# A hybrid layer kernel: the gate tiles of the GLA stage as pairs of seven products

## The chip, the cores and the metric

One core of a Trainium2 chip runs the whole program. The metric is the device time of one execution in microseconds (us); the median of three executions is taken.

## The reference, cut to what matters

One layer of a hybrid model for 320 tokens (256 of a prompt, 64 of a sample), all in float32. The input projection feeds three mixers (GLA, RWKV-7, Mamba-2) and three gates; the gated outputs are merged, projected, normalised and go through 64 experts.

```python
u = x @ w_in
u_gate, u_gla, u_rwkv, u_ssm = _split(u, (N_GATE, GLA_PROJ, RWKV_PROJ, SSM_PROJ))
o_gla, s_gla = _gla_mixer(u_gla, st_gla, gla_wa2, gla_ba, gla_norm_g)
...
g = jax.nn.sigmoid(u_gate.astype(jnp.float32)).reshape(b, l, 3, d)
merged = g[:, :, 0] * (o_gla @ gla_wo) + g[:, :, 1] * (o_rwkv @ rwkv_wo) + g[:, :, 2] * (o_ssm @ ssm_wo)
```

## The kernel before

The product `x @ w_in` is cut into NT = 115 tiles of 128 features by 320 tokens. The first 32 tiles are made ahead of the mixers, 28 of them as 14 pairs of seven products each (`project_pair`, L740): a 2 by 2 block scheme in which a pair of tiles takes seven block products of four 128x160 matmuls, not eight. GpSimd forms the sums of weight blocks for it (`weight_sums`), ScalarE copies four 160-column blocks out of the accumulators (`keep`), and VectorE adds the other blocks to them. The other tiles are made directly, as eight matmuls of 320 columns, between the steps of the mixers ("fill"), and ScalarE copies each whole tile out and stores it (`move`, L1463). The tile numbers run on: N_G0 = 96 to 98 are made between the Mamba-2 and the GLA stage, and the last 16 (99 to 114, all of them gate tiles) in the GLA stage.

The GLA stage (`gla(c)`, once in each of the engine programs) works through five chunks of 64 tokens, c = 0 to 4. Chunks 0 to 3 each carry four fill tiles; chunk 4 carries parts of the merge (`merge_part`, L1129). For one chunk:

- TensorE makes the pre-activation of the decays (L1065), turns the values (L1069), fills, makes and turns the scores' inputs (L1083, L1086), reads the state (L1093), applies the scores (L1101, signals `mixed`), makes the state's update (L1107), fills, and sums the squares for the norm (L1114).
- ScalarE copies the values (VT), moves a tile, then Exp and Ln of a softplus, three Exp for the decays (`decays`), moves a tile, Silu of the output gate, moves two tiles, and takes the square root of the norm (`root`, L1440).
- VectorE forms softplus's input, then its output (T4), a scan along the tokens (L2282), the difference EE (signals `gl_cs`), the scaled queries and keys (`gl_ops`), the masked scores (`gl_scm`), a copy and square of the output, the state (`gl_state`), the variance with a reciprocal (L2312), and five operations that normalise and gate the output (`gl_out`).
- SyncE loads the rows of the next chunk and the weights of a fill tile as soon as the slot's last tile is done.
- GpSimd forms six token sums for the merge at the start of the stage (`token_sums`, L2842 to L2846) and has nothing else there.

Each engine runs its own list in the written order and waits on semaphores. The order in which TensorE has its fill and the chunk's work is written out by hand:

```python
for f in range(3):
    fill(f)
...
pe.wait_ge(sem("gl_ops"), one)
...
last.then_inc(sem("state_sums"), 1)
fill(3)
```

## Time and profile before

| what | value |
|---|---|
| median of 3 executions | 1448.37 us (1446.8 to 1448.46) |
| the profiled execution's own time | 1444.06 us |
| its span | 1442.0 us |
| granted TensorE clock | 0.999 of full |
| busy: TensorE, VectorE, ScalarE, GpSimd | 98%, 50%, 29%, 16% |
| GLA stage, first TensorE work of chunk 0 | at 631.55 us |
| merge_part of chunk 4 begins | at 726.84 us |

The chain of work that ended last is followed back from the last instruction: each of its pieces released the next one. A piece on an engine other than TensorE is time in which TensorE had to wait. Busy shares are means over stages with different limits.

### The profile page before, as it was taken

What the parts mean: (1) busy time and instruction counts of PE and PEld (TensorE: products, weight loads), DVE (VectorE), ACT (ScalarE), POOL (GpSimd) and SP (SyncE); (2) the same over time, 40 slices, a digit from 0 to 9 for tenths busy, and PEclk for the clock granted to TensorE, in tenths of its full rate; (3) what the DMA queues carried; (4) which work ended last, traced back from release to release, by engine and by line L of the source; (5) the groups of instructions that cost most, each with busy time, mean ns of one, the idle gap of its engine ahead of it and who ended that gap; (6) DMA issues with size and microseconds to landing.
All of it is one profiled execution on the core that took longest, in us unless ns stands there. A gap on an engine that the chain in (4) does not pass through costs nothing.

```text
span 1442.0 us, 32350 instructions
## 1 busy us (share of the span) xinstructions
PE 1415.1 (98%) x13523; PEld 1024.3 (71%) x13523; DVE 724.3 (50%) x1360; ACT 411.3 (29%) x847; POOL 234.9 (16%) x193
## 2 busy tenths in 40 slices
PE   7999999999999999999999999999999999999997
PEld 6999777677777777667779985864476766757752
DVE  7443778887754677735458654623311112211217
ACT  2332543443432554434533211111111111111112
POOL 3784113230110111130013000011010000000000
PEclk9999999999999999999999999999999999999999
DMA  7796473744254444566568639699999999999996
GB/s 284 191 197 151 136 214 100 216 167 132 81 136 127 139 136 120 185 184 192 159 231 216 217 116 386 241 407 407 427 425 429 427 427 428 428 427 428 429 408 273
DMA packets 158017, 375.73 MB, mean 261 GB/s; under 512 B 102320, under 2 KB 110944, under 8 KB 139952
## 3 DMA queue, kind: packets, MB, share of 16 engines
q1 hardware_dynamic: 142048, 346.63, 67.2%
q0 software_dynamic: 7152, 16.85, 3.4%
q10 hardware_dynamic: 8672, 10.20, 2.0%
q8 instruction: 105, 1.72, 0.5%
q14 instruction: 40, 0.33, 0.1%
HBM read 329.22 MB, written 51.95 MB: 264 GB/s over the span
## 4 chain that ended last, share of the span: by engine, by line
PE 85%; DVE 6%; DMA 2%; ACT 2%; DVEq 2%; issue 1%; SPq 1%; ACTq 1%
PE PS L733 19%; PE PS L1303 15%; PE PS L1322 8%; PE PS L750 7%; PE PS L1149 6%; PE PS L1270 6%; PE PS L817 3%; PE PS L1129 2%; DVE region L1831 2%; PE PS L1191 2%; PE PS L1275 2%; DVE region L1838 2%; PE PS L1213 1%; DMA region<-projected 1%; PE PS L825 1%
## 5 line engine op out<-in xcount | busy, mean ns | idle before, releaser
L733 PE MATMUL PS<-h0T,region 128*128 128x320 f32 x1360 | 390.2, 439 | 2.0 <-issue 1.7
L1435 ACT ACTIVATE region<-PS 128x320 f32<-128x320 f32 (+5 forms) x351 | 145.7, 426 | 676.8 <-PE PS L733 237.6
L733 PEld LDWEIGHTS PS<-h0T,region 128*128 128x128 f32 x1360 | 251.2, 190 | 111.7 <-issue 15.0
L1303 PE MATMUL PS<-region 128*64 128x512 f32 x1024 | 228.1, 592 | 0.0
L1303 PEld LDWEIGHTS PS<-region 128*64 128x64 f32 x1024 | 117.6, 137 | 101.6 <-issue 49.8
L1831 DVE TENSOR_TENSOR region<-region 128x512 f32<-128x512 f32 (+10 forms) x237 | 165.3, 717 | 34.1 <-DMA region<-expert_rows 5.0
L1435 ACT ACTIVATE region<-region 128x256 f32<-128x256 f32 (+10 forms) x229 | 99.5, 465 | 83.0 <-DVEq L1854 13.7
L1322 PE MATMUL PS<-region,history 128*64 128x512 f32 x512 | 119.2, 597 | 1.1 <-ACTq L1771 0.5
L1831 DVE TENSOR_TENSOR history<-region,PS 128x256 f32<-128x256 f32 x32 | 13.5, 421 | 199.7 <-ACTq L1766 199.7
L1435 ACT ACT_TABLE_LOAD x77 | 98.8, 1283 | 25.3 <-ACTq L1482 9.8
L1838 DVE SCALAR_TENSOR_TENSOR region<-region,feature_vectors 128x320 f32<-128x320 f32 (+1 forms) x103 | 77.2, 750 | 53.2 <-ACTq L1511 41.0
L1270 PEld LDWEIGHTS PS<-region,h 128*128 128x128 f32 x736 | 85.8, 192 | 16.1 <-issue 15.9
L1270 PE MATMUL PS<-region,h 128*128 128x128 f32 x736 | 92.0, 278 | 0.0
L2565 DVE COPY region<-PS 128x512 f32<-128x512 f32 x32 | 22.1, 690 | 121.2 <-PE PS L1286 101.6
L1322 PEld LDWEIGHTS PS<-region,history 128*64 128x64 f32 x512 | 52.6, 137 | 42.5 <-issue 20.7
L1149 PE MATMUL PS<-region 128*128 128x160 f32 x528 | 73.8, 299 | 0.0
L1149 PEld LDWEIGHTS PS<-region 128*128 128x128 f32 x528 | 72.5, 190 | 0.2
L1435 ACT ACTIVATE region<-PS,region 128x512 f32<-128x512 f32 (+1 forms) x35 | 24.5, 699 | 146.7 <-PE PS L1322 146.4
L750 PE MATMUL PS<-region 128*128 128x160 f32 x448 | 65.4, 299 | 0.0
L750 PEld LDWEIGHTS PS<-region 128*128 128x128 f32 x448 | 62.4, 190 | 0.0
L1831 DVE TENSOR_TENSOR region<-region,PS 128x160 f32<-128x160 f32 (+3 forms) x95 | 43.3, 488 | 34.4 <-PE PS L750 14.7
L817 PEld LDWEIGHTS PS<-region 64*64 64x64 f32 x2720 | 49.8, 134 | 14.9 <-issue 12.7
(250 smaller groups left out, 1576.2 us busy)
## 6 DMA issues: line engine op xcount, KB each, us to landing
region<-moe_w SPq DMA_DIRECT2D x65, 2048.0 KB, 30.3
region<-moe_w SPq DMA_DIRECT2D x65, 1024.0 KB, 29.3
region<-w_in SPq DMA_DIRECT2D x115, 512.0 KB, 5.7
region<-wo SPq DMA_DIRECT2D x32, 512.0 KB, 4.3
expert_rows<-region SPq DMA_DIRECT2D x20, 512.0 KB, 7.2
region<-expert_rows SPq DMA_DIRECT2D x5, 2048.0 KB, 17.3
projected<-region ACTq DMA_DIRECT2D x59, 167.5 KB, 4.0
region<-projected SPq DMA_DIRECT2D x10, 768.0 KB, 6.8
```

The lines of the kernel that those rows point to most:

```text
L733: last = mm(PS[:, 6 + i % 2, 0:NTOK], WR[:, i, k, :], H0T[:, k, :], start=(k == 0), stop=(k == KT - 1))
L750: last = mm(out, lhs(k), rhs(k), start=start and k == 0, stop=k == KH - 1, skip_group_check=True)
L817: last = mm(head(out(j), 1 - x if across and j > 3 else x), head(lhs(j), x), head(rhs(j), x), **kw)
L1129: last = mm(PS[:, b, 0:NTOK], WR[:, i, k, :], OT[:, 8 * q + k, :], start=(k == 0 and q < 3), stop=(k == KT - 1 and q != 2))
L1149: last = mm(out, lhs(k), rhs(k), start=start and k == 0, stop=k == KH - 1, skip_group_check=True)
L1191: last = mm(PS[:, 2 * t + h, :], MG[:, k, t * 128:t * 128 + 128], WOUT[:, k, h * 512:h * 512 + 512], start=(k == 0), stop=(k == KT - 1))
L1270: last = mm(bank(h, 4, 128)[:, k], H0[:, t, (4 * h + k) * 128:(4 * h + k) * 128 + 128], OH[:, p, t, :], start=(h == 0 and k == 0 and t == ...
L1303: last = mm(PS[tiles(i), 2, :], XE[:, k, tiles(i)], W13[r][i][:, k * 512:k * 512 + 512], start=(k == 0), stop=(k == KT - 1))
L1322: last = mm(PS[tiles(i), 5 + h, :], HIDT[:, f, tiles(i)], W2[r][i][:, f * D + h * 512:f * D + h * 512 + 512], start=(f == 0), stop=(f == 1))
L1435: return nc.scalar.activation(out, in_, f, **kw)
L1831: return dve.tensor_tensor(out, a, b, op)
L1838: return dve.scalar_tensor_tensor(out=out, in0=a, scalar=s, in1=b, op0=op0, op1=op1)
```

## The change

The 16 gate tiles of the GLA stage become GATE_PAIRS = 8 pairs of seven products, two pairs in each of the chunks 0 to 3.

- TensorE: `gate_pair(g, first, end)` issues products first to end of pair g. Products 1, 3 and 6 go to block X (bank 6), 2 and 4 to Z (first half of bank 7), 5 and 7 to W (its second half); there is one set of blocks, so each pair waits for VectorE to have read the last one's. In a chunk, products 1 to 6 of the even pair stand behind L1065, product 7 and products 1 to 5 of the odd pair behind L1069, and products 6 and 7 of the odd pair behind L1107. Products 1 and 2 of pair 0 stand ahead of the chunk's first step.
- ScalarE: each `move` of a tile is replaced by copies of 160 columns (`keep_gate`), four to a pair. Two stand ahead of the root, which is moved from the end of its chunk into the next one, two behind softplus's Exp, two behind the decays, two ahead of Silu. The copy of VT moves behind the decays.
- VectorE: three adds to a pair (`gate_first`, `gate_rest`, `gate_last`). The last block of the even pair is added between T4 and the scan. Softplus's input of the next chunk (`gate_decays(c + 1)`) is formed ahead of the wait for the root.
- GpSimd: sums of weight blocks for each pair (`gate_sums`, four operations of 512 columns), with the token sums of the merge behind those of pair 1 and pair 3. A copy of the token sums TSUM into GTOK (2560 columns) is added in the first chunk of the Mamba-2 stage.
- SyncE: loads two tiles at a time, one pair's tiles once the slots are free, and issues the stores too, which ScalarE issued before. Tiles 99 and 100 are loaded ahead of the stage.

```diff
+        GTOK = take(4, KT // 2, NTOK // 2)
+        GSUM = [take(4, KT // 2, 128) for _ in range(2)]
...
-            weights((N_GLA - 1) // RING, (N_GLA - 1) % RING)
+            for n in range(N_GLA - 1, N_GLA + 2):
+                weights(n // RING, n % RING)
...
+            def gate_weights(g):
+                n = gate_tiles(g)[0]
+                for m in (n, n + 1):
+                    weights(m // RING, m % RING)
+            def gate_stores(g):
+                n, a, b = gate_tiles(g)
+                sp.wait_ge(sem("added_out"), 3 * g + 3)
+                for m, i in ((n, a), (n + 1, b)):
+                    sp.dma_start(ut[TILE[m], :, :, :], STG[:, i, :, :]).then_inc(sem(f"store_done{i}"), 16)
...
             gla_rows(0)
-            gla_weights(0)
+            gate_weights(1)
             gla_rows(1)
-            for c in range(1, NPC):
-                gla_rows(c + 1)
-                gla_weights(c)
+            for c in range(NPC - 1):
+                gate_weights(2 * c + 2)
+                gate_stores(2 * c)
+                gate_weights(2 * c + 3)
+                gla_rows(c + 2)
+                gate_stores(2 * c + 1)
...
+            def gate_pair(g, first, end):
+                p = PAIRS + g
+                n, a, b = gate_tiles(g)
+                X, Z, W = gate_blocks()
+                def product(k, out, lhs, rhs, start):
+                    for j in range(KH):
+                        last = mm(out, lhs(j), rhs(j), start=start and j == 0, stop=j == KH - 1, skip_group_check=True)
+                        if k == 5 and j < 2:
+                            last.then_inc(sem("tile_done"), 1)
+                    last.then_inc(sem("quad"), 1)
+                for k in range(first, end + 1):
+                    if k == 1:
+                        for m, i in ((n, a), (n + 1, b)):
+                            pe.wait_ge(sem(f"weights_in{i}"), (m // RING + 1) * 16)
+                        if g > 0:
+                            pe.wait_ge(sem("added_out"), 3 * g - 1)
+                        else:
+                            pe.wait_ge(sem("tile_moved"), N_GLA + 2)
+                        product(k, X, lambda j: WR[:, a, j, :], lambda j: H0H[:, j, 0], True)
+                    if k == 2:
+                        if g > 0:
+                            pe.wait_ge(sem("added_out"), 3 * g)
+                        product(k, Z, lambda j: WR[:, b, KH + j, :], lambda j: GTOK[:, 3, j], True)
+                    if k == 3:
+                        pe.wait_ge(sem("weights_summed"), p + 1)
+                        pe.wait_ge(sem("quad_kept"), 4 * p + 1)
+                        product(k, X, lambda j: GSUM[g % 2][:, 1, j], lambda j: GTOK[:, 1, j], False)
+                    if k == 4:
+                        pe.wait_ge(sem("quad_kept"), 4 * p + 2)
+                        product(k, Z, lambda j: WR[:, a, KH + j, :], lambda j: H0H[:, KH + j, 0], True)
+                    if k == 5:
+                        product(k, W, lambda j: GSUM[g % 2][:, 0, j], lambda j: GTOK[:, 0, j], True)
+                    if k == 6:
+                        pe.wait_ge(sem("quad_kept"), 4 * p + 3)
+                        product(k, X, lambda j: GSUM[g % 2][:, 2, j], lambda j: GTOK[:, 2, j], False)
+                    if k == 7:
+                        pe.wait_ge(sem("quad_kept"), 4 * p + 4)
+                        pe.wait_ge(sem("added_out"), 3 * g + 1)
+                        product(k, W, lambda j: GSUM[g % 2][:, 3, j], lambda j: H0H[:, KH + j, 1], False)
...
+                if c is not NPC:
+                    gate_pair(2 * c, 1 if c > 0 else 3, 6)
...
+                if c is not NPC:
+                    gate_pair(2 * c, 7, 7)
+                    gate_pair(2 * c + 1, 1, 5)
...
-                fill(3)
+                if c is not NPC:
+                    gate_pair(2 * c + 1, 6, 7)
...
+            def keep_gate(g, made, x):
+                act.wait_ge(sem("quad"), 7 * (PAIRS + g) + made)
+                a_(GKEPT[:, x].rearrange("p (c w) -> p c w", c=NCH), tuple(gate_blocks())[(0, 0, 1, 2)[x]], ACT.Copy)
+                act.drain().then_inc(sem("quad_kept"), 1)
             def gla(c):
-                def fill(f):
-                    if c is not NPC:
-                        move(c * (FILL_G // RING) + (N_GLA + f) // RING, (N_GLA + f) % RING)
-
-                one = c + 1
+                one, pairs = c + 1, c is not NPC
...
-                act.wait_ge(sem("gl_out"), one)
-                act.wait_ge(sem("gl_v"), 2 * NCH + one)
-                a_(VT, bank(1, 4, 128), ACT.Copy)
-                act.drain().then_inc(sem("gl_vt"), 1)
-                fill(0)
+                if pairs:
+                    keep_gate(2 * c, 1, 0)
+                    keep_gate(2 * c, 2, 2)
+                if c > 0:
+                    root(RG4, "variance", NCH + c, "rstd")
                 act.wait_ge(sem("softplus_in"), NCH + one)
                 a_(LB4, AB4, ACT.Exp, scale=-1.0)
-                act.drain()
+                if pairs:
+                    keep_gate(2 * c, 3, 1)
+                    keep_gate(2 * c, 5, 3)
+                else:
+                    act.drain()
                 a_(LB4, LB4, ACT.Ln, bias=1.0)
                 act.drain().then_inc(sem("softplus_out"), 1)
                 act.wait_ge(sem("gl_cs"), one)
...
                 a_(EE, EE, ACT.Exp, scale=1.0 / 16)
                 act.drain().then_inc(sem("decays"), 1)
-                fill(1)
+                if pairs:
+                    keep_gate(2 * c + 1, 1, 0)
+                    keep_gate(2 * c + 1, 2, 2)
+                act.wait_ge(sem("gl_out"), one)
+                act.wait_ge(sem("gl_v"), 2 * NCH + one)
+                a_(VT, bank(1, 4, 128), ACT.Copy)
+                act.drain().then_inc(sem("gl_vt"), 1)
+                if pairs:
+                    keep_gate(2 * c + 1, 3, 1)
+                    keep_gate(2 * c + 1, 5, 3)
                 a_(RR, UG[:, 16:24, :], ACT.Silu)
                 act.drain().then_inc(sem("gate_silu"), 1)
-                fill(2)
-                fill(3)
-                root(RG4, "variance", NCH + one, "rstd")
+                if c is NPC:
+                    root(RG4, "variance", NCH + one, "rstd")
...
-            def gla(c):
-                one = c + 1
+            def gate_decays(c):
                 dve.wait_ge(sem("gl_pre"), c * 2 + 1)
                 tt(T4, bank(0, 4, L, n=256), vec(V_BA, 4, L), add)
                 dve.drain()
                 stt(AB4, T4, -1.0, T4, mul, mx)
                 dve.drain().then_inc(sem("softplus_in"), 1)
+            def gate_first(g):
+                p, (n, a, b), (X, Z, W) = PAIRS + g, gate_tiles(g), gate_blocks()
+                dve.wait_ge(sem("quad_kept"), 4 * p + 4)
+                dve.wait_ge(sem(f"store_done{a}"), (n // RING + 1) * 16)
+                tt(quad_out(a, 0), GKEPT[:, 0].rearrange("p (c w) -> p c w", c=NCH), Z, add)
+                dve.drain().then_inc(sem("added_out"), 1)
+            def gate_rest(g):
+                p, (n, a, b), (X, Z, W) = PAIRS + g, gate_tiles(g), gate_blocks()
+                dve.wait_ge(sem("quad"), 7 * p + 6)
+                dve.wait_ge(sem("quad_kept"), 4 * p + 4)
+                dve.wait_ge(sem(f"store_done{b}"), ((n + 1) // RING + 1) * 16)
+                tt(STG[:, b, :, HIST:CW].rearrange("p c (j w) -> p j c w", j=2), GKEPT[:, 2:4].rearrange("p x (c w) -> p x c w", c=NCH),
+                   X.unsqueeze(1).to_broadcast([128, 2, NCH, L // 2]), add)
+                dve.drain().then_inc(sem("added_out"), 1)
+            def gate_last(g):
+                p, (n, a, b), (X, Z, W) = PAIRS + g, gate_tiles(g), gate_blocks()
+                dve.wait_ge(sem("quad"), 7 * p + 7)
+                tt(quad_out(a, 1), GKEPT[:, 1].rearrange("p (c w) -> p c w", c=NCH), W, add)
+                dve.drain().then_inc(sem("added_out"), 1)
+            def gla(c):
+                one, pairs = c + 1, c is not NPC
+                if pairs:
+                    gate_first(2 * c)
+                    gate_rest(2 * c)
                 dve.wait_ge(sem("softplus_out"), NCH + one)
 
...
+                if pairs:
+                    gate_last(2 * c)
                 flat = lambda x: x.rearrange("p a b -> p (a b)")
                 dve.tensor_tensor_scan(flat(CS4), CON[:, C_RST:C_RST + 4 * L], flat(T4), 0.0, mul, add)
                 dve.drain()
...
                 dve.drain().then_inc(sem("gl_ops"), 1)
+                if pairs:
+                    gate_first(2 * c + 1)
                 dve.wait_ge(sem("gl_pre"), c * 2 + 2)
...
                 dve.wait_ge(sem("state_sums"), NCH + one)
                 tt(SG, SG, banks(1, 2, 4, 256), add)
                 dve.drain().then_inc(sem("gl_state"), 1)
+                if pairs:
+                    gate_rest(2 * c + 1)
+                    gate_last(2 * c + 1)
                 dve.wait_ge(sem("square_sums"), NCH + one)
...
                 dve.reciprocal(RG4, RG4)
                 dve.drain().then_inc(sem("variance"), 1)
+                if pairs:
+                    gate_decays(c + 1)
...
+            gate_decays(0)
...
+                if c == 0:
+                    pool.tensor_copy(GTOK, TSUM)
+                    pool.drain()
...
-            for q in (0, 2):
-                token_sums(q)
+            def gate_sums(g):
+                n, a, b = gate_tiles(g)
+                S1, S2, S3, S4 = (halves(GSUM[g % 2][:, x]) for x in range(4))
+                A11, A12, A21, A22 = (halves(WR[:, i, k * KH:k * KH + KH, :]) for i in (a, b) for k in range(2))
+                for m, i in ((n, a), (n + 1, b)):
+                    pool.wait_ge(sem(f"weights_in{i}"), (m // RING + 1) * 16)
+                if g > 1:
+                    pool.wait_ge(sem("quad"), 7 * (PAIRS + g - 1))
+                ptt(S1, A21, A22, add)
+                ptt(S3, A11, A21, sub)
+                pool.drain()
+                ptt(S2, S1, A11, sub)
+                pool.drain()
+                ptt(S4, A12, S2, sub)
+                pool.drain().then_inc(sem("weights_summed"), 1)
+            for g in range(GATE_PAIRS):
+                gate_sums(g)
+                if g in (1, 3):
+                    token_sums(g - 1 if g == 3 else 0)
```

## Rows read from the trace of the kernel before

**Rows 1.** page, part 1: busy us of each engine (share of the span) and instructions.

```profile
PE 1415.1 (98%) x13523; PEld 1024.3 (71%) x13523; DVE 724.3 (50%) x1360; ACT 411.3 (29%) x847; POOL 234.9 (16%) x193
```

**Rows 2.** chain that ended last, GLA stage: start us, us, engine, what it made, line.

```profile
624.47 6.84 DMA region<-projected
...
631.55 0.69 PE PS L1065 x16
...
656.53 13.12 PE PS L733 x48
...
672.02 1.06 PE PS L1107 x8
673.09 4.50 PE PS L733 x16
677.59 0.86 PE PS L1114 x4
...
679.07 0.88 PE PS L1069 x16
679.94 13.12 PE PS L733 x48
...
726.84 13.12 PE PS L1129 x48
```

**Rows 3.** timeline of chunk 1: start us, us, engine, line, operation [idle before, releaser].

```profile
661.96 1.28 ACT L1435 ACT_TABLE_LOAD   x1 [0.45 <-ACTq L1482]
...
663.73 1.28 ACT L1435 ACT_TABLE_LOAD   x1
...
665.99 0.69 DVE L2282 TENSOR_TENSOR_SCAN region<-constants,region 128x256 f32<-128x256 f32 x1
...
667.24 1.03 ACT L1435 ACTIVATE region<-region 128x256 f32<-128x256 f32 x3 [0.43 <-DVEq L2285]
...
668.66 0.75 DVE L1831 TENSOR_TENSOR region<-region 128x256 f32<-128x256 f32 x2
...
669.57 0.31 PEld L1083 LDWEIGHTS PS<-region 128*64 128x64 f32 x8 [0.44 <-DVEq L2291]
...
672.86 2.04 DVE L1831 TENSOR_TENSOR region<-region 128x512 f32<-128x512 f32 x2
...
674.98 1.22 DVE L1831 TENSOR_TENSOR region<-region,PS 128x1024 f32<-128x1024 f32 x1
...
678.99 1.75 DVE L2312 RECIPROCAL region<-region 128x256 f32<-128x256 f32 x1
```

**Rows 4.** the same chain where pairs of seven products run, 14 and 12 pairs.

```profile
34.71 106.49 PE PS L750 x784
...
766.37 91.28 PE PS L1149 x672
```

**Rows 5.** timeline where pairs run: matmuls, a copy, an add.

```profile
96.48 2.34 PE L750 MATMUL PS<-region 128*128 128x160 f32 x16
96.69 0.30 ACT L1435 ACTIVATE region<-PS 128x160 f32<-128x160 f32 x1 [2.96 <-PE PS L750]
...
103.21 0.32 DVE L1831 TENSOR_TENSOR region<-region,PS 128x160 f32<-128x160 f32 x1 [0.16 <-PE PS L750]
```

**Rows 6.** issues of the fill tiles' weights, 606 to 704 us.

```profile
DMA to landing us min/median/max: 5.0/6.5/7.8
```

**Rows 7.** timeline, end of the Mamba-2 stage: the last three direct tiles and a token sum.

```profile
617.25 13.16 PE L733 MATMUL PS<-h0T,region 128*128 128x320 f32 x48 [0.26 <-ACTq L1482]
...
622.72 1.54 POOL L2842 TENSOR_TENSOR region<-region 128x640 f32<-128x640 f32 x1 [7.93 <-DVEq L376]
```

**Rows 8.** timeline, VectorE with and without GpSimd beside it.

```profile
178.49 2.01 DVE L1831 TENSOR_TENSOR region<-region,constants 128x512 f32<-128x512 f32 x1
178.72 1.23 POOL L2771 TENSOR_TENSOR region<-region,feature_vectors 128x512 f32<-128x512 f32 x1
...
202.56 0.69 DVE L1831 TENSOR_TENSOR region<-region,constants 128x512 f32<-128x512 f32 x1
```

More of the change, by code:

```diff
@@ L39 @@
 UNITS = 12
+GATE_PAIRS = 8
 UNIT_ORDER = (0, 2, 3, 1)
@@ L209, in quad_sum, with gate_tiles, gate_blocks @@
             return shaped(PS[:, b, 0:NTOK // 2], NCH, L // 2)
+        def gate_tiles(g):
+            n = N_GLA + 2 * g
+            return n, n % RING, (n + 1) % RING
+        def gate_blocks():
+            return (shaped(PS[:, b, o:o + NTOK // 2], NCH, L // 2) for b, o in ((6, 0), (7, 0), (7, NTOK // 2)))
         def kept(u, x):
@@ L232, in hybrid_layer @@
         RG = take(4, L)
+        ssm_end = at[0]
         assert at[0] <= REGION.shape[1], at[0]
@@ L245, in hybrid_layer @@
         UAS = (UA, UA2)
+        at[0] = mixer_end + 24 * L
+        GKEPT = take(4, NTOK // 2)
+        gates_at = 31872
+        assert at[0] <= 27776 and ssm_end <= gates_at
+        at[0] = gates_at
+        GTOK = take(4, KT // 2, NTOK // 2)
+        GSUM = [take(4, KT // 2, 128) for _ in range(2)]
+        assert at[0] <= 36864 + 768 + KT * 128
         at[0] = mixer_base
@@ L567, in gla_rows @@
                 sp.dma_start(UGS[c % 2], ut[T_GLA:T_GLA + 24, :, c, HIST:CW].rearrange("t p w -> p t w")).then_inc(sem(landed), 16)
-            def gla_weights(c):
-                for f in range(FILL_G):
-                    weights(c * (FILL_G // RING) + (N_GLA + f) // RING, (N_GLA + f) % RING)
+            def gate_weights(g):
[7 more added lines that the diff above has]
+                    sp.dma_start(ut[TILE[m], :, :, :], STG[:, i, :, :]).then_inc(sem(f"store_done{i}"), 16)
             def gla_out(s):
@@ L600, in _ @@
                 mixer_weights(0, n % RING, n + 1)
+                if n == NT - RING + 1:
+                    gate_stores(GATE_PAIRS - 2)
+            gate_stores(GATE_PAIRS - 1)
             gla_out(0)
@@ L1070, in gla @@
                 last.then_inc(sem("gl_v"), 1)
-                for f in range(3):
-                    fill(f)
+                if c is not NPC:
+                    gate_pair(2 * c, 7, 7)
+                    gate_pair(2 * c + 1, 1, 5)
                 if c is NPC:
-                    pe.wait_ge(sem("tile_moved"), NT + 1)
+                    pe.wait_ge(sem("added_out"), 3 * GATE_PAIRS)
                     merge_part(0, 0, 7)
-                    pe.wait_ge(sem("tile_moved"), NT + 2)
                     merge_part(0, 2, 6)
@@ L1660, in _ @@
                 move(n // RING, n % RING)
+            def keep_gate(g, made, x):
+                act.wait_ge(sem("quad"), 7 * (PAIRS + g) + made)
+                a_(GKEPT[:, x].rearrange("p (c w) -> p c w", c=NCH), tuple(gate_blocks())[(0, 0, 1, 2)[x]], ACT.Copy)
+                act.drain().then_inc(sem("quad_kept"), 1)
             def gla(c):
-                def fill(f):
-                    if c is not NPC:
-                        move(c * (FILL_G // RING) + (N_GLA + f) // RING, (N_GLA + f) % RING)
-                one = c + 1
+                one, pairs = c + 1, c is not NPC
                 act.wait_ge(sem(gla_in(c)[0]), gla_in(c)[1])
                 UG = UGS[c % 2]
-                act.wait_ge(sem("gl_out"), one)
-                act.wait_ge(sem("gl_v"), 2 * NCH + one)
-                a_(VT, bank(1, 4, 128), ACT.Copy)
-                act.drain().then_inc(sem("gl_vt"), 1)
-                fill(0)
+                if pairs:
[3 more added lines that the diff above has]
+                    root(RG4, "variance", NCH + c, "rstd")
                 act.wait_ge(sem("softplus_in"), NCH + one)
                 a_(LB4, AB4, ACT.Exp, scale=-1.0)
-                act.drain()
+                if pairs:
[3 more added lines that the diff above has]
+                    act.drain()
                 a_(LB4, LB4, ACT.Ln, bias=1.0)
@@ L1705, in keep_unit @@
             def keep_unit(u, made, x, region):
-                act.wait_ge(sem("quad"), 7 * (PAIRS + u) + made)
+                act.wait_ge(sem("quad"), 7 * (PAIRS + GATE_PAIRS + u) + made)
                 a_(UKEPT[u % 2][:, 160 * x:160 * x + 160], region, ACT.Copy)
@@ L2348, in unit_sums @@
             def unit_sums(u):
-                p = PAIRS + u
+                p = PAIRS + GATE_PAIRS + u
                 ring, (a, b), _ = unit_weights(u)
@@ L2834, in _ @@
                 pool.drain().then_inc(sem("squares_summed"), 1)
+                if c == 0:
+                    pool.tensor_copy(GTOK, TSUM)
+                    pool.drain()
             meet(pool, 3)
```

8 lines of the change are left out of this document (4 added, 4 removed).

## The prediction, made before the change was run

> **What bounds the kernel now.** I read the page first, then the chain of waits, then the timeline of one GLA chunk. The page shows TensorE busy for 98% of the span [rows 1], so a saving on it counts wherever nothing else takes its place. The chain through the GLA stage is almost all TensorE [rows 2]: one chunk's three fill tiles begin at 656.53, the next chunk's at 679.94, a period of 23.41 us. Of it 13.12 + 4.50 = 17.6 us are the four tiles and 5.8 us the chunk's own steps. But the timeline shows a second chain right behind: VectorE ends the operations before `gl_ops` at 668.66 + 0.75 = 669.41, and TensorE's first weight load after its three tiles starts at 669.57, put down to them [rows 3]. ScalarE and VectorE have almost no slack against 13.12 us of fill. The question is therefore not only what the products save, but which hand-overs the shorter fill still hides.
>
> **What the products save.** A direct tile takes 13.12 / 3 = 4.37 us [rows 2], a pair of tiles 8.75. Seven products take 106.49 / 14 = 7.61 us and 91.28 / 12 = 7.61 us where pairs run elsewhere, 1.09 a product [rows 4]. That is 1.14 us a pair, 2.3 a chunk, 9.1 us over eight pairs if TensorE never waits. Nothing else moves off TensorE.
>
> **A steady chunk, step by step.** Zero is the start of L1107 (672.02 in chunk 1 [rows 2]). A hand-over from TensorE to a copy takes 0.21, the copy 0.30, its signal 0.05 [rows 5], and TensorE starts 0.16 after a signal [rows 3].
>
> 1. L1107 (1.06), products 6 and 7 of the odd pair (2.17) and L1114 (0.86) end at 4.1. The next L1065 waits for the state. Square and decayed state end at 674.90, the state's add runs 674.98 to 676.20 [rows 3], that is 4.18, plus 0.16: 4.34. Loss 0.2. Before, the 4.50 us tile hid this.
> 2. L1065 ends at 4.96, product 1 at 6.05, product 2 at 7.13. ScalarE's second copy is out at 7.7.
> 3. Now ScalarE has the root and softplus's Exp ahead of the third copy. Both need a table load, and loads follow the last operation directly, then the operation: one load to the next is 1.77 us [rows 3]. Two of them end at 11.24; the third copy's signal is at 11.6, TensorE can start product 6 at 11.75. It ended product 5 at 4.96 + 5 x 1.09 = 10.4. Loss 1.35. VectorE's variance is no cause: its adds and the 1.75 us reciprocal [rows 3] end near 7.6, ahead of the root.
> 4. Products 6, L1069 (0.88), 7: to 14.8. The add of the last block waits for product 7 (0.2) and takes 0.32 [rows 5]; the scan starts at 15.4. From the scan's start to the end of the three Exp was 665.99 to 668.27, 2.28 us [rows 3]: 17.7. Only then does ScalarE copy the odd pair's first block: signal at 18.05, product 3 at 18.2. Products 1 and 2 had ended at 17.0. Loss 1.2.
> 5. Products 3 to 5 (3.26) and L1083 to L1101 (2.38 before, from the end of the 13.12 us to 672.02 [rows 2]) end at 23.85. VectorE's `gl_ops` come near 18.9, hidden; `gate_first` ahead of the masked scores ends before L1086 does.
>
> So the period is 23.85 where it was 23.41: 2.3 us saved, 2.75 lost to the three waits. ScalarE's copies by themselves are cheap (8 x 0.30 against four copies and stores) and its issue of stores goes to SyncE; it is their place in its list that costs. SyncE's stores wait for `added_out`, with the loads of the next odd pair and of rows behind them. These weights land 5.0 to 7.8 us after issue [rows 6] and are wanted some 15 us after, so I price SyncE's new order at nothing; without that cover each late load would be TensorE's wait one to one.
>
> **Entry and exit.** Tile 98 ends at 630.4 and L1065 started at 631.55, after the rows had landed at 631.3 [rows 2, 7]. Now tile 98 is copied out (631.1) and products 1 and 2 run ahead, to 633.3. Up to L1107 there are then L1065, ten more products (10.9), L1069, the loss at product 3 (1.25) and the 2.38: 649.3, where chunk 0 had 648.6. That is +0.7. Three steady periods (chunk 0 to 3) give 3 x 0.44 = +1.3. Out of chunk 3 the merge began 7.92 after L1107 (679.94 less 672.02, the same in each chunk [rows 2]); now it is 4.34 + 0.62 + 0.88 = 5.84: -2.1. Chunk 4's own chain is hidden by 13.12 us of merge [rows 2], since its root no longer follows any copy. Sum so far: -0.1 us.
>
> **GpSimd beside VectorE.** Before, GpSimd had only the token sums, at the start of the stage. Now it has 32 operations of 512 columns in it. A VectorE operation with both inputs in SBUF took 2.01 us where a GpSimd one ran 178.72 to 179.95 beside it, and 0.69 alone [rows 8]: it ended 0.55 after GpSimd's, +1.3 us. Adds that read PSUM kept their 0.32 [rows 5]. The Trainium skill ("GPSIMD Engine Reference", Specifications) says the same and more: VectorE's two-port modes, which have one SBUF input, contend too. By that rule the two scaling operations of the normalisation would be hit as well, and the sum below would be some 0.6 higher.
>
> Where do the hits lie on the path? Weights of the next even pair are issued at product 5 (9.6 after zero) and land 6.5 later [rows 6], at 16.1, against scan and difference at 15.4 to 16.7; a pair's sums last about 5.3 us. I take half a hit, 0.6, in chunk 1 and in chunk 2; chunk 3 has none. In chunk 0 the sums of pair 1 (weights from 637, until 642.5) lie on scan and difference (from 640.9): 1.3. Then come three token sums of 1.54 [rows 7] and pair 2's sums, until about 652.5, on the square and the decayed state of chunk 0, which now set the next L1065: 1.3. The token sums behind pair 3 lie on the normalisation of chunk 0's output, ahead of `gate_first` of chunk 1: 0.7. Sum 4.5. Bounds: 0, if every hit falls into slack, and 9, if a hit goes through two GpSimd operations in a row (S1 and S3 have no gap between them). I take 4.5, since the row shows the hit plainly and its places are on the path, and the two bounds lie equally far.
>
> The copy into GTOK (2560 columns on GpSimd in the Mamba-2 stage) has no row of its length. Five times the 512-column rows is 6 us [rows 8]; it stands where GpSimd is idle until its next turn. Between 0 and one hit (1.3) is its cost; I take 0, the operations on the path there read PSUM.
>
> **Sum.** -0.1 + 4.5 = +4.4 us. The profiled execution took 1444.06 for a span of 1442.0, 4.3 below the median of 1448.37. Against its own time the sum is 1448.5, against the median 1452.8. I give the latter. About 0.2% (2.9 us) is what a measurement of this kernel can tell from no change.
>
> **Rivals.**
>
> - *The waits, without the hits* (0.27). GpSimd's sums fall into slack, up to a microsecond of them counts: 1448.3 to 1449.3. For it: 2.4 us of slack on `gl_ops`, and the second batch of sums in a steady chunk meets operations that read PSUM. Against it: chunk 0, where sums and token sums queue up for 15 us.
> - *Longer hits* (0.10). Each goes through two GpSimd operations: +9, 1457.
> - *Faster: ScalarE is in time for product 6* (0.14). If the root's table load ran ahead of the first two copies, in the time in which ScalarE waits for them, the third copy would come at 10.3, and the loss of 1.35 would go in three chunks: -4.1, so 1444.2 without hits. For it: ScalarE is idle then. Against it: in the trace loads stand right ahead of their operation, behind the copies [rows 3]. It decides the sign from 0.9 us less loss a chunk on, if the hits are absent too. All losses gone would be -9.1, 1439.3, which no row supports.
> - *The forecast* (0.45), with its own range of 1450.5 to 1455.5.
>
> The rest (0.04) I leave to places that I have not seen, on the slow side.
>
> Faster by over 0.2%: 0.14. Within 0.2%: the second case less a part that it gives to the slow side, plus a little of the forecast's lower end: 0.28. Slower: 0.58. The range goes from 1446.5, which leaves out the faster case, to 1457.5, which takes in the longer hits' estimate.
>
> **What would show each step.** In the changed profile the products' line should be about 1.09 us a product; TensorE's idle time should stand ahead of the product's matmuls with ScalarE as its releaser, some 1.2 us four times and 1.35 three times, and 0.2 ahead of L1065 with VectorE. The period of chunk 3 should be near 23.9 and those of chunks 1 and 2 longer. The merge should begin near 731 against 726.84. Scan, difference or the decayed state should show over 1 us where they had 0.42 to 0.69 or 1.22. The prediction is wrong if the idle time at product 6 is missing (table loads placed elsewhere), if VectorE's operations keep their lengths (no hits), or if TensorE waits for weights.

## The result, and the profile after

The changed kernel took **1460.07 us** (median of 4 runs, 1458.64 to 1460.9) against 1447.59 before (4 runs, 1444.44 to 1448.46): ratio **1.0089, 95% interval 1.0071 to 1.0108**. It is slower by 12.5 us, where +4.4 was forecast; 1460 lies above the forecast's range. The profiled execution took 1460.9 for a span of 1459.1.

Part 1 of the page, which answers to [rows 1]:

```profile
PE 1414.4 (97%) x13715; PEld 1041.1 (71%) x13715; DVE 746.8 (51%) x1384; ACT 413.6 (28%) x863; POOL 278.8 (19%) x226
```

TensorE's busy time is where it was (1415.1 before), in a span 17 us longer. Of these 17 us 2.4 stand ahead of the GLA stage, in this pair of profiles: 0.7 of them before any changed work (the row of 64 matmuls at 448.82 before starts at 449.48 here), and in the second profiles of both kernels (experiments 11 and 12) the stage starts only 0.4 us apart. I don't count them to the change. To place the loss I measure the *stage*: from the end of tile 98 to the start of chunk 4's merge. It was 96.4 us before (630.41 to 726.8); now it is 109.1 (632.80 to 741.9), +12.7. The period from one state update to the next (L1107 before, L1183 now) was 23.4 three times and is 28.07, 27.87 and 24.66.

The chain of waits of the changed kernel, chunks 1 and 2 (L1094 the products, L1183 the state update, L1139 the old L1065, L1512 ScalarE, L1922, L1926 and L2405 VectorE's adds, scalings and scan):

```profile
665.10 1.27 DVE region L1922
...
668.13 1.47 DVE region L1926
...
671.32 1.34 PE PS L1094 x8
...
673.13 1.51 DVE region L2405
...
674.72 1.25 DVE region L1922
...
677.63 3.50 PE PS L1094 x24
...
683.51 1.07 PE PS L1183 x8
684.58 2.37 PE PS L1094 x16
686.95 0.86 PE PS L1191 x4
...
687.87 0.69 PE PS L1139 x16
...
688.57 2.43 PE PS L1094 x16
...
691.41 1.28 ACT L1512
...
693.21 1.28 ACT L1512
...
695.18 1.35 PE PS L1094 x8
...
699.32 1.51 DVE region L2405
...
700.92 1.26 DVE region L1922
...
703.83 5.17 PE PS L1094 x24
```

Before, this chain was TensorE's almost alone [rows 2]. Now it leaves TensorE at two of the places that the prediction named: two table loads ahead of product 6 (it starts at 695.18, 11.67 after the zero of 683.51; 11.75 was forecast), and scan, difference and Exp ahead of product 3 of the odd pair. Three things differ from the forecast. Scan and difference take 1.51 and 1.26 in *both* chunks, against 0.69 [rows 3] and 0.42; half of one such hit was forecast for a chunk. The normalisation ahead of `gate_first` is stretched by more than the 0.7 forecast (1.27 and 1.47 at 665 to 669.6), and holds TensorE to 671.32. And the three products at 703.83 take 5.17 us, those at 677.63 3.50; nothing of that was forecast.

Here are chunk 3's rows of the same chain, where no sums of GpSimd are left:

```profile
727.19 0.69 DVE region L2405
...
727.96 0.42 DVE region L1922
...
730.17 3.50 PE PS L1094 x24
```

The granted clock (the first column after the engines' busy times), in stretches around three products each:

```profile
647.90:653.10 5.20, 5.20 (x26) 5.03 (x28) 2.03 (x3) 1.13 (x3) 4.83 (x4) 0.67 0.05 9
677.60:681.10 3.50, 3.46 (x26) 3.33 (x26) 1.69 (x2) 1.17 (x3) 1.07 (x1) 1.00 0.01 2
703.80:709.00 5.20, 5.17 (x26) 5.03 (x28) 1.68 (x2) 1.17 (x3) 1.07 (x1) 0.67 0.00 0
```

Twice TensorE ran part of the three products at its lower level (a mean of 0.67 between 1.2 and 2.4 GHz), behind 2.40 and 2.81 us without work; once, behind 2.81 too, it didn't. Each fall cost 1.67 us.

Behind the stage there is one more difference, at the first unit of the mixer (L1226):

```profile
785.41 3.53 PE L1226 MATMUL PS<-region 128*128 128x160 f32 x24 [1.76 <-DVEq L2495]
```

### The profile page after: what moved, and what is told of

Its sections match the earlier page's. It is cut to its first block, busy times and chain, and to the rows that moved or that the text cites. A ratio compares the mean times of both kernels' runs of the same rounds, so it can differ in the third digit from the quotient of the medians.

```text
span 1459.1 us, 32888 instructions
## 1 busy us (share of the span) xinstructions
PE 1414.4 (97%) x13715; PEld 1041.1 (71%) x13715; DVE 746.8 (51%) x1384; ACT 413.6 (28%) x863; POOL 278.8 (19%) x226
## 3 DMA queue, kind: packets, MB, share of 16 engines
q8 instruction: 107, 1.75, 0.5%
## 4 chain that ended last, share of the span: by engine, by line
PE 82%; DVE 8%; ACT 3%; DMA 2%; DVEq 2%; issue 1%; SPq 1%; ACTq 1%
PE PS L766 15%; PE PS L1380 15%; PE PS L1399 8%; PE PS L783 7%; PE PS L1226 6%; PE PS L1347 6%; PE PS L1094 3%; DVE region L1922 3%; PE PS L850 3%; PE PS L1268 2%; PE PS L1352 2%; DVE region L1929 2%; PE PS L1290 1%; ACT region L1512 1%; ACT L1512 1%
## 5 line engine op out<-in xcount | busy, mean ns | idle before, releaser
L1512 ACT ACTIVATE region<-PS 128x160 f32<-128x160 f32 (+6 forms) x367 | 148.3, 415 | 673.9 <-PE PS L766 207.6
L766 PE MATMUL PS<-h0T,region 128*128 128x320 f32 x1104 | 319.3, 439 | 2.4 <-issue 2.1
L766 PEld LDWEIGHTS PS<-h0T,region 128*128 128x128 f32 x1104 | 203.1, 190 | 91.2 <-issue 14.0
L1922 DVE TENSOR_TENSOR region<-region 128x512 f32<-128x512 f32 (+10 forms) x237 | 173.8, 752 | 35.7 <-DMA region<-wo 5.9
L1512 ACT ACTIVATE region<-region 128x256 f32<-128x256 f32 (+10 forms) x229 | 99.5, 465 | 93.7 <-DVEq L2408 14.3
L1922 DVE TENSOR_TENSOR history<-region,PS 128x256 f32<-128x256 f32 x32 | 13.5, 421 | 199.0 <-ACTq L1857 199.0
L1347 PEld LDWEIGHTS PS<-region,h 128*128 128x128 f32 x736 | 85.8, 192 | 16.1 <-issue 15.9
L1922 DVE TENSOR_TENSOR region<-region,PS 128x160 f32<-128x160 f32 (+4 forms) x119 | 52.3, 466 | 58.5 <-ACTq L1743 16.4
L1226 PE MATMUL PS<-region 128*128 128x160 f32 x528 | 74.1, 299 | 1.8 <-DVEq L2495 1.8
L1226 PEld LDWEIGHTS PS<-region 128*128 128x128 f32 x528 | 72.5, 190 | 2.2 <-DVEq L2495 2.0
L1512 ACT ACTIVATE region<-PS,region 128x512 f32<-128x512 f32 (+1 forms) x35 | 24.5, 699 | 146.7 <-PE PS L1399 146.4
L3032 POOL DMA_INDIRECT expert_rows<-region,row_index x21 | 20.6, 983 | 233.1 <-DVEq L2728 233.1
```

The source lines that it names most:

```text
L766: last = mm(PS[:, 6 + i % 2, 0:NTOK], WR[:, i, k, :], H0T[:, k, :], start=(k == 0), stop=(k == KT - 1))
L1226: last = mm(out, lhs(k), rhs(k), start=start and k == 0, stop=k == KH - 1, skip_group_check=True)
L1347: last = mm(bank(h, 4, 128)[:, k], H0[:, t, (4 * h + k) * 128:(4 * h + k) * 128 + 128], OH[:, p, t, :], start=(h == 0 and k == 0 and t == ...
L1512: return nc.scalar.activation(out, in_, f, **kw)
L1922: return dve.tensor_tensor(out, a, b, op)
```

## The experiments

My theory after the result: of the 12.7 us of the stage, most is GpSimd's sums beside VectorE's short chain, with the lower clock behind the longer waits, and the rest the order of ScalarE's copies. The rival: the order of the work alone (copies behind table loads, the chunk's first products behind L1139), with GpSimd beside the point. Line numbers of the variants lie a few above those of the changed kernel.

**1. No sums by GpSimd from pair 2 on** (the sums of pairs 0 and 1 are used for all, so the gates are not the reference's), and **2. no sums at all** (nor are the ones of pairs 0 and 1 made; the token sums stand at the stage's start).

```diff
+                if g > 1:
+                    nc.gpsimd.sem_inc(sem("weights_summed"), 1)
+                    return
```

> This kernel leaves out GpSimd's sums of weight blocks for the pairs 2 to 7 (it waits for the weights and signals at once; TensorE multiplies by the sums of pairs 0 and 1), so the gates are not the reference's; everything else keeps its place. Read the GLA stage alone, from the end of the last direct tile to the start of chunk 4's merge: 96.4 us before, 109.1 in the changed kernel. Theory (GpSimd's sums stretch VectorE's two-input operations, and these lie on the path): in chunks 1 and 2 the scan and the difference go from 1.51 and 1.26 us back to 0.69 and 0.42, the stage falls by 1.65 twice, and the clock's dip in chunk 2 goes as well (1.7): 104.1. Rival (the stretching has another cause, the order on ScalarE say): both operations stay at 1.5 and 1.26 and the stage at 109.

> This kernel leaves out all of GpSimd's sums of weight blocks (the places hold other numbers, copied there in the Mamba-2 stage) and has the token sums at the stage's start as the kernel before, so that GpSimd does nothing beside VectorE from chunk 0's middle on. Theory (ScalarE's order costs about 1.3 us a period, the rest is GpSimd): all periods fall to that of chunk 3 of the changed kernel, 24.7 us, the first part to 19.5 (22.6 less 1.2 for the stretched operations and 1.9 for the clock): stage 99.4 against 109.1, so 9.7 of the 12.7 us are GpSimd's and 3.0 ScalarE's order. Rival (the hits fall into slack and the order on ScalarE costs it all): stage 107 or more.

Measured: 1451.21 and 1450.50 us; the kernel before took 1446.7 beside them. The stages are 100.4 and 99.3 us, all periods 24.54 to 24.67, and no clock below 1.00 around the products. Each of the runs up to the sixth is one execution; I read them by the stage in its profile. In the second run other numbers stand in the places of the sums, so its gates aren't the reference's either. The rival falls. All but 3 us of the 12.7 go with the sums, the clock's part among them. The first came out better than expected (100.4, not 104) for two reasons: TensorE was idle for 2.27 us in chunk 0, behind the one stretched difference that was left, and its clock held (1.7); and with no sums of pairs 2 and 3 ahead of them the token sums were over at 661.4, before the normalisation, which was no longer stretched (1.9).

**3. Third copy ahead of softplus's Exp, 4. the odd pair's first copy ahead of the decays, 5. both.**

```diff
+                if pairs:
+                    keep_gate(2 * c, 3, 1)
                 act.wait_ge(sem("softplus_in"), NCH + one)
...
+                if pairs:
+                    keep_gate(2 * c + 1, 1, 0)
                 act.wait_ge(sem("gl_cs"), one)
```

> One thing is moved: ScalarE's third copy of the even pair stands between the root and softplus's Exp, not behind the Exp. Theory (product 6 waits only because one more table load stands ahead of that copy; but what ends the chunk is the scan, behind T4): TensorE's wait ahead of product 6 falls from about 1.3 us to nothing in chunks 2 and 3, product 7 comes 1.2 earlier, yet T4 comes 0.35 later, so the scan gains only some 0.5: the wait ahead of product 3 of the odd pair grows by 0.7, and a period falls by 0.5. Stage 107.5. Rival (a wait taken away is worth its length): a period falls by 1.3, stage 105.

> One thing is moved: ScalarE's first copy of the odd pair stands ahead of its wait for the scan (gl_cs), not behind the three Exp of the decays. Theory (product 3 of the odd pair waits for that copy alone): the wait ahead of product 3 goes, product 4 waits for the second copy, 1.1 us of the wait are won in each of four chunks, and TensorE's longest idle stretch falls from 2.6 to 1.5 us, so that the two dips of the clock go (1.7 and 1.9): stage 109.1 - 4.4 - 3.6 = 101.1. Rival (the dips do not come from the idle time): they stay, stage 104.7. Second rival (the chain of VectorE ends the chunk anyway): the wait moves to L1159 and the stage stays at 109.

> Both moves of ScalarE's copies together: the third copy of the even pair ahead of softplus's Exp, the first copy of the odd pair ahead of the wait for the scan. Alone they gave a stage of 106.1 and 103.9 us against 109.1. Theory (each removes another wait of TensorE, and what is left are VectorE's stretched operations): the gains add, stage 101. Rival (one chain through scan and decays holds both, so the second move finds the same wait): 103 or more.

Measured: 1457.71, 1455.56 and 1451.79 us; stages of 106.1, 103.9 and 101.8. The waits that the prediction ascribed to ScalarE's list are ScalarE's: without sums beside it (chunk 3) the period is 23.64 with the one copy moved, 24.46 with the other, and 23.25 with both, 1.4 less than in the changed kernel. While the sums lie on VectorE's chain the gain is less regular (28.73 in chunk 1 of the first, where the clock fell behind a wait of 3.05), since the waits go to the next hand-over. None of the three came out as forecast. The first took 1.0 off the clean period, between my 0.5 and the rival's 1.3. The second was worse than I expected (101, measured 103.9): the falls of the clock went, but the copy gave 0.2 in the clean chunk and not 1.1, because product 4 of the odd pair then waited for the second copy (1.05 us, and 1.6 beside the sums). The third was expected at 101.

**6. Only GpSimd's work moved**: the even pairs' sums wait for `gl_ops`, the odd pairs' for `gl_state`, the token sums for the state of chunk 3.

```diff
+                    if g % 2 == 0:
+                        pool.wait_ge(sem("gl_ops"), g // 2)
+                    else:
+                        pool.wait_ge(sem("gl_state"), (g + 1) // 2)
...
-                if g in (1, 3):
-                    token_sums(g - 1 if g == 3 else 0)
+            pool.wait_ge(sem("gl_state"), NPC + 1)
+            for q in (0, 2):
+                token_sums(q)
```

> The changed kernel with GpSimd's work moved in time alone: the sums of an even pair wait for gl_ops (scan and decays are over), those of an odd pair for gl_state, the token sums for the state of chunk 3. Theory (what costs is where the sums meet VectorE, not that they are there): scan and difference keep 0.69 and 0.42 us in chunks 1 and 2, the square and decayed state grow by about 1 us in chunks 0 to 2; of the 9.8 us that went with all sums left out, some 6 come back: stage 103.5. Rival (two engines at work cost the same wherever the sums are put): stage 108 or more.

Measured: 1451.21 us, stage 99.5, periods 24.55, 24.54 and 24.67. I had expected 103.5, with square and decayed state stretched; they kept 2.04, since the even pair's sums were over (676.84) before the square began (677.45). The same work of GpSimd, done elsewhere in the chunk, costs 0.2 us against no sums at all (99.3, run 2). Its chain in chunk 2 reads as chunk 3 of the changed kernel did:

```profile
692.42 0.69 DVE region L2405
...
693.19 0.42 DVE region L1922
...
695.28 3.50 PE PS L1094 x24
```

**7. Both copies, the odd pair's second copy too, and the sums moved. 8. As 7, with VectorE making S1 and S3 of the even pairs**, GpSimd S2 and S4, and VT's transposes right behind L1139.

> Third copy of the even pair ahead of Exp, first and second copy of the odd pair ahead of the scan's wait, and GpSimd's sums placed as in the run before. Theory: TensorE waits only for the state at a chunk's start (by 1.0 us, since the even pair's sums lie on the square and the decayed state) and in chunk 0, a period is 21.4 + 0.8 for the starts of groups + 0.8 = 23.0, stage 17.9 + 3 x 23.0 + 5.9 = 93, that is 3 us less than before the change, and the time 1446 to 1447 against some 1447.5. Rival (gl_ops come late, hit by the same sums): the wait moves to L1159, a period is 24 and the time is 1450.

> As the run before, with two more steps: VectorE makes two of the four sums of an even pair between gl_ops and its masked scores (GpSimd the other two), and TensorE turns the values right behind L1139, so that products 6 and 7 stand together. Theory: GpSimd's part no longer lies on the decayed state (0.8 us a period less) and one start of a group less (0.2): period 22.0, stage 90 to 91, time 1444. Rival (VectorE's two sums delay the masked scores by more than they save): period 23 or more, a wait ahead of L1177.

Measured: 1449.25 us (10 runs; ratio to before 1.0007, interval 0.9995 to 1.0019) and 1452.59 (6 runs; 1.0033, 1.0018 to 1.0047). I had expected periods near 23 and 22; they are 24.19 three times, and 24.71, 25.05, 23.74. VectorE and TensorE in the timeline of run 7:

```profile
698.29 0.45 PE L1159 MATMUL PS<-region 128*64 128x64 f32 x8 [0.72 <-DVEq L2415]
...
706.56 0.69 PE L1139 MATMUL PS<-region 128*64 128x64 f32 x16 [1.52 <-DVEq L2434]
```

```profile
701.58 3.51 DVE L1923 TENSOR_TENSOR region<-region 128x512 f32<-128x512 f32 x2
```

Square and decayed state took 3.51 us together where they had 2.04 [rows 3], with the even pair's sums beside them, and L1139 waits for the state behind them. The earlier copies had shortened the chunk so far that this became the path. The wait at L1159 has another cause: the second copy now stands ahead of the decays' table load. In run 8 VectorE's own two sums (1.29 us for both) are put into the chain directly: TensorE waits 0.90 us at L1177, ahead of which they stand, as that run's rival had it. Both are misses.

**9. Run 5 with the sums moved as in run 6. 10. The same, with the last four stores issued by ScalarE.**

```diff
-                if n == NT - RING + 1:
-                    gate_stores(GATE_PAIRS - 2)
-            gate_stores(GATE_PAIRS - 1)
...
+            act.wait_ge(sem("added_out"), 3 * GATE_PAIRS)
+            for g in (GATE_PAIRS - 2, GATE_PAIRS - 1):
+                n, a, b = gate_tiles(g)
+                for m, i in ((n, a), (n + 1, b)):
+                    act.dma_start(ut[TILE[m], :, :, :], STG[:, i, :, :]).then_inc(sem(f"store_done{i}"), 16)
```

> Third copy ahead of the softplus Exp and the odd pair's first copy ahead of the decays (as in the run with both copies moved), the odd pair's second copy behind the decays as in the changed kernel, and GpSimd's sums in the slack (even pairs' once KET's operands are made, odd pairs' once the state is updated). Theory: without hits of GpSimd every period is what the last one of the run with both copies was, 23.25 us, so the stage is 95.5 us (99.5 less three times 1.3) and the time about 1448.3: within 0.2% of the kernel before. Rival: the even pair's sums, which stretched the square and the decayed state in the run with three copies moved, come onto the path here too: periods of 24.2 and more, stage 98, time 1450 or more.

> The run above with one thing more: the four stores of the last two pairs are issued by ScalarE at the start of chunk 4 instead of by SyncE among the loads of wo. Theory: the wait of 1.6 to 1.8 us at the first unit's third product comes from gate rows that land 1.0 us later because they share SyncE's queue with the stores; with the stores on ScalarE's queue the first gate rows land within 4.0 to 4.3 us of issue again and the time is 1.0 to 1.7 us below the run above, about 1447. Rival: the wait stays within 0.3 us, since it comes of GpSimd's token sums beside VectorE's unit sums and of where the loads meet other transfers; the time is the same as above within 0.3.

Measured: run 9 took **1447.93 us** (12 runs, 1446.43 to 1449.71) against 1449.6 before beside it (23 runs): ratio 0.9986, interval 0.9974 to 0.9998. Its median is the lowest of the variants (run 10 is as good within the noise), 12 us below the changed kernel and level with the one before (the gain of 0.14% is less than the 0.2% that I count). Its stage is 96.5 us (95.5 expected), its periods 23.66 (23.25 expected; square and decayed state take 2.44 there for 2.04, beside the end of the even pair's sums). The timeline of TensorE in one period of it:

```profile
669.23 1.35 PE L1094 MATMUL PS<-h0T,region 128*128 128x160 f32 x8 [1.05 <-ACTq L1743]
...
678.80 0.69 PE L1139 MATMUL PS<-region 128*64 128x64 f32 x16 [0.46 <-DVEq L2435]
```

What is left are 1.05 us for the odd pair's second copy and 0.46 for the state. They, and the group starts (below), take back the 2.3 us that the products save in a chunk. Run 10 took 1448.13 (12 runs; 0.9990, 0.9978 to 1.0001): the wait at the first unit is still 1.62 us, and the first six loads of gate rows still take 4.59 us to issue where they took 4.00. My theory of the shared queue falls.

**11. The changed kernel and 12. the kernel before, each unaltered and profiled again.**

> The changed kernel unaltered, profiled a second time. Theory: the lower clock of TensorE behind the idle time ahead of the third product of the odd pairs belongs to this order of work and comes back at two of the same three places (0.67 over the first three products), and the stretched scan and difference are again 1.5 and 1.26 us long in chunks 1 and 2. Rival: where the clock falls is chance; then it falls elsewhere or not at all, and the stage is up to 3.4 us shorter, about 106 us.

> The kernel before unaltered, profiled a second time. Theory: its first profile was of an execution some 3 us below its median, and the difference lies outside the GLA stage; here too the stage (end of tile 98 to the merge of chunk 4) is 96.4 us with periods of 23.4, but the unit sums start later and TensorE waits 1 to 2 us at the first unit, as in every profile of a changed kernel, so that this wait isn't the change's. Rival: the first unit starts without a wait again, and the wait of 1.6 to 1.8 us belongs to the change.

Measured: 1459.37 and 1447.76 us. The changed kernel's stage is 108.9, its scan and difference 1.51 and 1.26 in chunks 1 and 2 again. The clock fell at one place only, the three products of chunk 2:

```profile
646.35:649.80 3.45, 3.45 (x26) 3.28 (x26) 2.04 (x3) 1.14 (x3) 3.22 (x3) 1.00 0.00 0
674.60:678.10 3.50, 3.50 (x26) 3.33 (x28) 1.66 (x2) 1.14 (x3) 1.04 (x1) 1.00 0.01 2
700.80:707.20 6.40, 6.39 (x24) 6.23 (x24) 1.66 (x2) 1.14 (x3) 1.04 (x1) 0.53 0.07 7
```

They took 6.46 us where 3.50 is usual. So the price (3.0 and 3.3 us a run) comes back, the place only in part. The kernel before has a stage of 99.2 us in its second profile, 2.8 more than in the first. Its chain of waits shows landings in it, of chunk 0's rows and of the weights of fill tiles:

```profile
624.94 7.72 DMA region<-projected
...
651.67 7.88 DMA region<-w_in
...
698.70 7.89 DMA region<-w_in
```

and its clock fell as well, behind 2.04 us without work at 632.91:

```profile
632.90:634.00 1.10, 1.09 (x19) 1.10 (x21) 0.00 (x0) 0.00 (x0) 0.25 (x1) 0.52 1.04 376
634.00:636.00 2.00, 2.00 (x18) 1.67 (x15) 0.85 (x2) 0.14 (x1) 0.00 (x0) 0.50 0.97 368
```

The rows' landing costs 0.9 more than in [rows 2], the clock 1.6 (the first tile began 2.8 behind L1065 where it was 1.5, and took 0.3 longer), the late weights 0.2 each. No profile of a changed kernel had a landing on the chain within the stage. At the first unit the kernel before waits 0.21 us in its second profile and not at all in its first; every changed kernel and variant waits 1.6 to 1.95 there. That wait belongs to the change, so the rival of run 12 held.

Over the two profiles of each, the stage costs 109.0 less 97.8, 11.2 us, and the first unit some 1.7: 12.9, against 12.5 between the medians.

## Why the prediction was wrong in size and right in direction

In its order:

- **What bounds the kernel**: right. The second chain, of VectorE and ScalarE, was the limit.
- **What the products save**: 1.09 us a product is right inside a group (products 1 to 5 behind L1139 run from 688.57 to 694.25, 5 x 1.09 and 0.23 more). Left out was the start: each group behind the chunk's own matmuls takes 0.2 to 0.26 more (1.35 and 1.30 for one, 2.37 and 2.43 for two, 3.50 for three). Three such starts lie on the path of a chunk, 0.7 us.
- **A steady chunk**: two of its three waits stood where they were put, with the releasers named, that for product 6 until 11.67 (11.75 forecast). The third, 0.2 for the state ahead of L1139, is hardly a wait: L1139 starts at 4.36 (4.34 forecast, from the state), but TensorE's own L1191 ended only at 4.30 and not at 4.1, because products 6 and 7 took 2.37 and not 2.17. The period without hits is 24.54 to 24.67, not 23.85; the starts and L1145 (1.02 for 0.88) make the 0.8. That is 2.2 us over three periods.
- **Entry and exit**: the exit is 5.91 (5.84 forecast). The entry was +1.7 in run 6 (+1.5 in run 2, which has no sums at all), not +0.7, from the same starts and the first chunk's waits.
- **GpSimd beside VectorE: the step that failed.** The run in which the sums only moved gives the term by itself: 109.1 less 99.5, 9.6 us for 4.5 forecast; 1.7 + 1.7 of it is the clock. The other 6.2 us are stretched operations: 1.1 in chunk 0 (1.3 + 1.3 forecast; the square's part didn't count), 1.9 at the normalisation (0.7), 1.6 and 1.7 in chunks 1 and 2 (0.6 and 0.6). I had let the sums start when their weights land, at 16.1 after the zero, halfway through scan and difference. But the weights land earlier (issued at 693.46 and 693.87, 3.5 and 4.3 us before landing, where I had 6.5), and what releases S1 is the end of the even pair's product 7: `gate_sums(g)` waits for the products of pair g - 2, whose sums it overwrites. VectorE's last add ahead of the scan waits for the same product. So the two meet in chunks 1 and 2 alike, by the way the waits are written; in chunk 2:

```profile
698.88 0.32 DVE L1922 TENSOR_TENSOR region<-region,PS 128x160 f32<-128x160 f32 x1 [1.09 <-PE PS L1094]
```

```profile
699.02 1.27 POOL L2998 TENSOR_TENSOR region<-region 128x512 f32<-128x512 f32 x1 [6.58 <-PE PS L1094]
700.25 1.64 POOL L2999 TENSOR_TENSOR region<-region 128x512 f32<-128x512 f32 x1
```

S1 and S3 follow each other without a gap, so that the scan (699.32 to 700.83) is held by the one and the difference (700.92 to 702.18) by the other. The prediction's upper bound had two sums in a row in view, but behind one operation of VectorE. In chunk 1's normalisation it is the token sums behind pair 3 (664.55 to 669.45), as forecast; they stretch its four operations by 3.3 us, and 1.9 of it reaches TensorE.
- **The clock** had no term at all. The prediction counted a wait as its own length; here waits of 2.4 to 2.8 us cost 1.7 to 3.0 more in the work behind them, though not each time. With 3.4 us it is the largest single part of what the forecast missed.
- **Weights and SyncE's order at nothing**: right. **GTOK's copy at nothing**: right; it took 2.32 us (6 was estimated), beside nothing on the path. The first unit's wait of 1.7 us was unpriced.
- **The rival "ScalarE in time for product 6"** is dead: the first load ran 0.06 behind the copy, the second stood ahead of product 6 in every chunk from 1 on.
- **The rule of the Trainium skill** ("GPSIMD Engine Reference", Specifications), that VectorE contends with GpSimd in its two-port modes too, was put at +0.6. The trace agrees that an operation with one tensor from SBUF can be held: the first scaling, at 668.13, took 1.47 us, and the two together 1.73 for 0.62 where GpSimd was idle, 1.1 more. The reciprocal has one as well and kept its 1.75 beside the sums; which mode either runs in, the trace doesn't show.

The sum as measured, on the same base: -0.1, + 2.2 (periods), + 1.0 (entry), + 6.2 (stretched operations), + 3.4 (clock) = 12.7 for the stage. Against the forecast's 4.4 that is 8.3 more: 5.1 from the meeting with GpSimd (1.7 in stretched operations, 3.4 in the clock behind the waits that they lengthened) and 3.2 from periods and entry. Of the rivals, "longer hits" (0.10, 1457) came nearest, 3 us short. The direction was right for the reasons given: even with no sums at all (run 2) the stage is 2.9 us longer than before.

**Open.** Why the gate rows of the mixer land later behind the changed stage: ScalarE's work on the first of them starts 5.3 to 5.9 us after their first issue in the twelve profiles of the changed kernel and its variants, 4.75 and 5.24 in the two of the kernel before. Run 10 speaks against the queue of the stores (5.37, and the wait at the first unit unchanged). That this costs 1.7 us is argued from the timelines, not tested: VectorE's three sums at 777.72 took 5.66 us, 4.58 in the kernel before, and start behind GpSimd's token sum (777.25) where they started ahead of it. All fourteen profiles fall on one side or the other: 4.58 and 4.59 where the three start ahead (by 0.51 and 0.02 us, both of the kernel before), 5.66 to 5.95 where they start behind (by 0.04 to 0.67).

```profile
777.72 5.66 DVE L1922 TENSOR_TENSOR region<-region 128x512 f32<-128x512 f32 x3 [0.19 <-issue]
```

```profile
777.25 1.68 POOL L2986 TENSOR_TENSOR region<-region 128x640 f32<-128x640 f32 x1 [1.91 <-PE PS L1206]
```

## What to carry to other kernels

When TensorE's cover over a chain of VectorE operations is cut, place GpSimd's work by waits in the part of the loop where VectorE has slack: the same sums cost 9.8 us in one place and 0.2 in another. Look at what releases the other engine's work: where it waits for the same product as the chain does, the two meet every time. Price such a meeting as one hit for each operation of the chain, not half a hit, and price a wait of over 2 us in a matmul-bound stage with the clock in mind. Count the hand-overs that a saving brings with it: here the best order of both lists gave back 2.3 us a loop in waits and starts, and came out level.

## What the hardware showed that I had not expected

- **The clock fell only behind longer waits, and not each time.** In the stage, over all runs, behind 2.04, 2.19, 2.40, 2.75, 2.81, 2.82 and 3.05 us without work the next matmuls ran in part at the lower level; behind 2.06, 2.27, 2.39, 2.81, 2.82 and 3.33 not. Where it fell, 1.1 to 3.0 us were lost. What else decides, no run here tells.
- **Which of the two engines starts first decides which is held.** VectorE operations with two tensors from SBUF, and the scalings, that began while a sum of GpSimd ran ended 0.15 to 0.55 us behind the end of one: 0.69 became 1.51, 0.42 became 1.26, 0.34 became 1.47. Where VectorE began first, it kept its length and GpSimd's sum (1.27 elsewhere) grew: in chunk 2 of run 3 the scan at 698.11 took its 0.69 and the sum at 698.13 took 1.73, and so in run 7:

```profile
686.42 0.42 DVE L1930 SCALAR_TENSOR_TENSOR region<-region 128x256 f32<-128x256 f32 x1
686.44 1.53 POOL L3008 TENSOR_TENSOR region<-region 128x512 f32<-128x512 f32 x1
```

[rows 8] doesn't fit: there VectorE began 0.23 ahead and was held all the same. Adds with a PSUM input kept 0.32 (643.36 in the changed kernel, beside a sum from 642.79 to 644.06), and the reciprocal its 1.75.
